# Delta stage of a two-layer block: order of the last output-gate projections and of the work beside them

## The reference, cut to what matters

```
qkv = silu(short_conv([q, k, v]))            # 8 heads, 128 wide each
o   = chunk_gated_delta(q, k, v, g, beta)    # forwards, and backwards
o   = rmsnorm(o_fwd + o_bwd, norm_w)
y_a = o * silu(z)                            # z: the output gate of the head
merged = sigmoid(gate_a) * (y_a @ w_pa) + sigmoid(gate_b) * (y_b @ w_pb)
```

## Time and profile before

| | us |
|---|---|
| runs: median of 3 (lowest to highest) | 3124.99 (3123.63 to 3127.92) |
| the profiled execution, its own time | 3120.17 |
| its span in the trace | 3118.3 |
| TensorE busy / VectorE / ScalarE / GpSimd in the span | 2972.4 / 1687.0 / 1468.2 / 423.7 |
| mean granted TensorE clock | 0.982 of full speed |

### The profile page before, as it was taken

How to read it: one execution, slowest core, us unless ns; L and a number is a source line. 1 busy time by engine, 2 the same in 40 slices (tenths; PEclk the granted TensorE clock), 3 DMA queues, 4 the chain that set the end, 5 groups by cost and what they waited for, 6 DMA issues and landing times. The chain is left out here.

```text
span 3118.3 us, 51224 instructions
## 1 busy us (share of the span) xinstructions
PE 2972.4 (95%) x20348; PEld 2380.8 (76%) x20348; DVE 1687.0 (54%) x2566; ACT 1468.2 (47%) x2859; POOL 423.7 (14%) x276
## 2 busy tenths in 40 slices
PE   7999989999999999899999989989999899899998
PEld 5788777777777788687777867777888777678887
DVE  6767743677447777625766445544344445444343
ACT  4555542656334555425665345644333356543332
POOL 1544510000014545300000000010000100010000
PEclk9999999999999999999999999989999999999999
DMA  3221112212222211122222222113222222122222
GB/s 133 76 74 67 47 62 96 73 59 71 84 88 78 83 62 64 41 94 74 71 71 78 95 65 98 48 55 106 97 94 94 81 72 75 36 93 94 94 95 80
DMA packets 41244, 243.12 MB, mean 78 GB/s; under 512 B 6672, under 2 KB 7632, under 8 KB 15440
## 3 DMA queue, kind: packets, MB, share of 16 engines
q1 hardware_dynamic: 41040, 240.30, 22.3%
HBM read 233.36 MB, written 2.20 MB: 76 GB/s over the span
## 5 line engine op out<-in xcount | busy, mean ns | idle before, releaser
L317 PE MATMUL bank<-hT,ws 128*128 128x512 f32 x2112 | 875.1, 414 | 38.1 <-DVE hT L508 26.0
L321 PE MATMUL bank<-hT,ws 128*128 128x512 f32 x2112 | 830.0, 393 | 0.0
L320 PE MATMUL bank<-hT,ws 128*128 128x512 f32 x2112 | 828.4, 392 | 0.0
L317 PEld LDWEIGHTS bank<-hT,ws 128*128 128x128 f32 x2112 | 400.4, 190 | 126.4 <-issue 48.0
L274 DVE TENSOR_TENSOR ws<-raw,ws 128x2048 fp32r<-128x2048 f32 x160 | 368.5, 2303 | 211.2 <-ACT ws L268 208.2
L268 ACT ACTIVATE ws<-raw 128x2048 fp32r<-128x2048 f32 x172 | 328.9, 1912 | 302.9 <-PE bank L317 181.7
L321 PEld LDWEIGHTS bank<-hT,ws 128*128 128x128 f32 x2112 | 399.0, 189 | 87.6
L320 PEld LDWEIGHTS bank<-hT,ws 128*128 128x128 f32 x2112 | 401.0, 190 | 69.1 <-issue 1.4
L946 PE MATMUL bank<-uS,ws 128*128 128x512 f32 x512 | 199.2, 389 | 0.0
L949 PE MATMUL bank<-uS,ws 128*128 128x512 f32 x512 | 199.2, 389 | 0.0
L950 PE MATMUL bank<-uS,ws 128*128 128x512 f32 x512 | 199.2, 389 | 0.0
(11 more groups left out here) (368 smaller groups left out, 4856.0 us busy)
## 6 DMA issues: line engine op xcount, KB each, us to landing
raw<-in_w_ff SPq DMA_DIRECT2D x64, 1024.0 KB, 4.7
raw<-in_w_delta SPq DMA_DIRECT2D x32, 1024.0 KB, 4.8
raw<-in_w_diff SPq DMA_DIRECT2D x32, 1024.0 KB, 4.8
raw<-in_w_att SPq DMA_DIRECT2D x20, 1024.0 KB, 4.8
raw<-in_w_merge_a SPq DMA_DIRECT2D x16, 1024.0 KB, 4.8
raw<-in_w_merge_b SPq DMA_DIRECT2D x16, 1024.0 KB, 4.8
raw<-in_w_out SPq DMA_DIRECT2D x16, 1024.0 KB, 5.0
rows<-sum_rows SPq DMA_DIRECT2D x16, 512.0 KB, 5.7
```

What stands on the lines that cost most here:

```text
L317: first = pe.matmul(out, hi, x[:, 0, k], start=(begin and k == steps[0]), stop=False)
L320: pe.matmul(out, hi, x[:, 1, k], start=False, stop=False)
L321: last = pe.matmul(out, lo, x[:, 0, k], start=False, stop=(end and k == steps[-1]))
```

## The change

It orders the 32 tiles of a layer anew: z of head 6 and z of head 7 become the last two, so that position 27 is q of head 7, 28 its k, 29 its v, 30 is z of head 6 and 31 z of head 7. The chunks of weights are packed on the host in this order, and waits and banks go by position (`DELTA_AT`). `ahead` is now 3 in cores 0 to 4, 2 in core 5, 1 in core 6, 0 in core 7. The fill of core 5 becomes 24 steps (v of head 6, q and k of head 7), that of core 6 stays at 16 (v of head 7, z of head 6), and that of core 7 begins with 8 steps of z of head 7. The first gate's steps then come in calls 9 to 16, calls 17 to 25 are empty, and the second gate has 26 to 33.

ScalarE applies Silu to z of head 6 in core 6 and not in core 5, and to z of head 7 in core 7, after level 3, between two loads of a table. The splits of the merge stage's first chunks move from level 0 to 2 on ScalarE and from level 1 to 3 on VectorE, in cores 6 and 7; in core 6 two steps of the convolution take the place at level 1.

```diff
+def delta_tiles():
+    tiles = [(h, j) for h in range(HEADS) for j in range(4)]
+    late = [(HEADS - 2, 3), (HEADS - 1, 3)]
+    return [x for x in tiles if x not in late] + late
+DELTA_TILES = delta_tiles()
+DELTA_AT = {hj: n for n, hj in enumerate(DELTA_TILES)}
...
+GATES_PAUSE = 8
...
-                core(i, i % 2, first=(i == 0), ahead=min(2, HEADS - 1 - i))
+                core(i, i % 2, first=(i == 0), ahead=min(3, HEADS - 1 - i))
...
                 def stream(i, ahead):
-                    if ahead:
+                    if ahead > 2:
                         yield from gemm(i + 1, (2, 3))
-                    if ahead > 1:
                         yield from gemm(i + 2, (0, 1))
-                    if not ahead:
+                    elif ahead > 1:
+                        yield from gemm(i + 1, (2, 3))
+                        yield from gemm(i + 2, (0,))
+                    elif ahead:
+                        yield from gemm(i + 1, (1, 2))
+                    else:
+                        yield from gemm(i, (3,))
                         yield from gates_ahead()
...
                         if x == KT - 1:
-                            for _ in range(2 * KT - 1):
+                            for _ in range(GATES_PAUSE):
                                 yield
...
-                        if a == 0:
-                            if ahead > 1:
-                                st.high(act, i + 2, 0)
-                            elif ahead:
-                                following.first_high(act, st)
-                            else:
-                                following.second_high(act)
+                        if a == 0 and ahead > 1:
+                            st.high(act, i + 2, 0)
+                        elif a == 2 and ahead == 1:
+                            following.first_high(act, st)
+                        elif a == 2 and not ahead:
+                            following.second_high(act)
...
                         if a == 3 and ahead:
                             decay_exp(i + 1)
                             act.preload_act_table_set(SILU)
+                        elif a == 3:
+                            act.preload_act_table_set(SILU)
+                            silu_z(i, p)
+                            act.preload_act_table_set(LN_EXP)
                     if ahead:
-                        silu_z(i + 1, 1 - p)
+                        if ahead > 2:
+                            silu_z(i + 1, 1 - p)
+                        elif ahead == 1:
+                            silu_z(i, p)
                         silu(i + 1, 1 - p, 0)
...
                             elif ahead:
-                                following.first_low(dve, st)
-                            else:
-                                following.second_low(dve)
+                                some(fill, 2)
...
-                            some(fill, 2)
+                            if ahead == 1:
+                                following.first_low(dve, st)
+                            elif not ahead:
+                                following.second_low(dve)
+                            else:
+                                some(fill, 2)
```

More of the change, by code:

```diff
@@ L380, in weight_chunks @@
             at = i * P
-            d.append(tile_pair(column_tile(w, (COL_QA + at, P)), column_tile(w, (COL_KA + at, P))))
-            d.append(tile_pair(column_tile(w, (COL_VA + at, P)), column_tile(w, (COL_ZA + at, P))))
             f.append(tile_pair(column_tile(w, (COL_QB + at, P)), column_tile(w, (COL_KB + at, P))))
@@ L386, in weight_chunks @@
             mb.append(tile_pair(column_tile(w, (COL_GB + at, P)), column_tile(pb, (at, P))))
+        tiles = [column_tile(w, ((COL_QA, COL_KA, COL_VA, COL_ZA)[j] + h * P, P)) for h, j in DELTA_TILES]
+        d += [tile_pair(tiles[n], tiles[n + 1]) for n in range(0, len(tiles), 2)]
         for n in range(0, KT, 2):
@@ L1440, in _, with gemm @@
                 st.credit(pe)
-                def gemm(h, js):
+                def gemm(g, js):
                     for j in js:
                         if j % 2 == 0:
-                            st.ready(pe, h, j // 2)
-                        if h > 0 or j >= 2:
-                            pe.wait_ge(taken, h * 4 + j - 1)
+                            st.ready(pe, g, j // 2)
+                        if g > 0 or j >= 2:
+                            pe.wait_ge(taken, g * 4 + j - 1)
                         for last in st.product(pe, B[j % 2][:, :], j // 2, j % 2, k.hT):
@@ L1665, in pad_copy @@
                 def pad_copy(h, j):
-                    act.wait_ge(tile, h * 4 + j + 1)
+                    n = DELTA_AT[h, j]
+                    act.wait_ge(tile, n + 1)
                     if h > 0:
                         act.wait_ge(conv_ready, (h - 1) * 3 + j + 1)
-                    act.activation(pad[:, j, 2:2 + SEQ], B[j % 2][:, :], ACT.Copy).then_inc(taken, 1)
+                    act.activation(pad[:, j, 2:2 + SEQ], B[n % 2][:, :], ACT.Copy).then_inc(taken, 1)
                 def silu(h, p, j):
@@ L1677, in silu_z @@
                 def silu_z(h, p):
-                    act.wait_ge(tile, h * 4 + 4)
-                    act.activation(zs[:, p], B[1][:, :], ACT.Silu).then_inc(taken, 1)
+                    n = DELTA_AT[h, 3]
+                    act.wait_ge(tile, n + 1)
+                    act.activation(zs[:, p], B[n % 2][:, :], ACT.Silu).then_inc(taken, 1)
                 def token_squares(h, p, j, core):
@@ L1840, in conv @@
                     for j in range(3):
-                        dve.wait_ge(taken, h * 4 + j + 1)
+                        dve.wait_ge(taken, DELTA_AT[h, j] + 1)
                         chain(dve.tensor_scalar(cv[:, j], pad[:, j, 0:SEQ], cw[:, j, 0:1], None, ALU.mult))
@@ L1872, in gate_out @@
                     dve.wait_ge(x_ready, scratch_use(use, core) + 1)
-                    dve.wait_ge(taken, h * 4 + 4)
+                    dve.wait_ge(taken, DELTA_AT[h, 3] + 1)
                     dve.scalar_tensor_tensor(yt, B[XB][:, :], pA[:, PA_GNW:PA_GNW + 1], zs[:, p], ALU.mult, ALU.mult).then_inc(x_taken, 1)
```

## The result

The median went from 3124.79 us (15 runs) to **3130.63 us** (15 runs, 3126.24 to 3138.06): a ratio of 1.0021, with a 95% interval of 1.0015 to 1.0028. The forecast was 3130.5 us. The change made the kernel slower: by 5.8 us or 0.19% between the medians, just inside the 0.2% that the prediction called no change.

A forecast was written before the change was run, and what follows sets the result against it. TensorE bounds cores 1 to 5, latency between VectorE, ScalarE and TensorE the thin stretches of cores 6 and 7. Per layer -1.5 + 0 + 4.2 = +2.7 us, +5.5 for two, gives 3130.5 us; range 3121 to 3138.

The forecast's parts named there:

- Core 5: Core 5 loses eight product steps and becomes 1.5 us shorter per layer, between 0 and 2.4.
- The wait on GpSimd: Core 5's tail: N waits behind GpSimd's low part and L1364, with 0.4 us in hand, so it costs nothing.
- Core 6: Core 6 keeps 16 steps; the moved split stays covered by product steps: 0, with 0.3 us either way.
- Core 7: Core 7 per layer: beginning 2.5 us longer, `widen` of level 4 1.95 later, L1601 of s = 1 0.25 sooner: 4.2 longer.
- The fourth merge step after the transposes: End of core 7: one merge step more follows the last transposes; adds 0, at most 0.4 us.
- the 0.25: Core 7: call 25 becomes empty, so L1601 of s = 1 goes when r is ready, 0.25 us sooner.
- The clock: TensorE's half-clock falls in thin stretches: filled levels 1 to 3 against thinner level 4 and core 5 tail cancel, 4 us either way.
- The slow rival: Core 7's level 4 stall loses the clock in both layers, plus a fall in core 5's tail: 3136.3 us; chance 0.30.
- The fall that it gave to core 5's tail: Part of the slower rival: a clock fall of 1.3 us in core 5's thin tail.
- The sign of being wrong: Half-clock stretches outweigh the terms of the sum; one of three signs named, no size given.
- The drain: Rival: each table switch in core 7 costs a 1.38 us drain beside its load, 5.6 us in all: 3136.1 us; chance 0.03.
- the fast rival: Filled levels keep the clock up in core 7 of both layers, 9.0 us back: about 3119.7 us; chance 0.12.

The follow-up runs named there:

- the idle products in the stall: The changed kernel with six 128x512 matmuls whose result nobody reads in the level 4 stall of core 7: 3126.8 us, 1.0008 of the kernel before.
- the row with four loads: The changed kernel with two more table loads behind the two at level 3 of core 7: 3138.7 us, 1.0041 of the kernel before.
- the loads moved: The changed kernel with Silu of z of head 7 and its two table loads moved to s = 2 of core 7: 3123.3 us, 0.9998.
- core 6 with 24 steps: The new tile order with core 5's eight steps moved to core 6, core 7 that of the kernel before: 3120.5 us, 0.9989.
- core 7 with thin levels: The kernel before, but core 7 has one product step before and one after `widen`, second gate straight after the first: 3118.8 us, 0.9974.

## Why the prediction was right

The forecast of 3130.5 us and the median of 3130.63 agree to 0.1 us, and that closeness is luck. The mechanism was right, but the terms of the sum were 1.1 us per layer too low together, and no run shows what made up for it.

**Core 5: -1.5 us forecast, -1.6 measured.** The bound from core 6's tail and the two ScalarE operations that core 6 lacks were the right ingredients. The wait on GpSimd was closer than the 0.4 us given. One of VectorE's small operations took 1.91 us and ended as GpSimd's low part did; N was ready 0.16 us ahead of its transposes (355.18 and 0.69, against 356.03). VectorE, layer 0, then TensorE:

```profile
350.71 1.91 DVE L1883 TENSOR_SCALAR odd<-odd 128x4 f32<-128x4 f32 x1
...
355.18 0.69 DVE L1936 TENSOR_TENSOR Nn<-Nn,cc 128x512 f32<-128x512 f32 x1
...
356.03 0.60 PE L1567 MATMUL bank<-cc,Nn 128*128 128x128 f32 x4
```

**Core 6: 0 forecast, +0.8 measured.** This is the term that was mis-sized, outside its 0.3. I weighed TensorE's cover for the moved split and not what GpSimd reads beside it.

**Core 7: 2.5 + 1.95 - 0.25 = 4.2 forecast, +4.6 at full clock** (48.96 with the idle products in the stall, against 44.33). The beginning is 19.50 us for 19.48, `widen` comes 3.81 us after its level for 3.8. Of the missing 0.4, some 0.26 lie at the end: from the start of VectorE's last low part to the merge stage it takes 1.80 us in the run with idle products for 1.54 (443.69 to 445.23). The fourth merge step after the transposes was given as 0 to 0.4 and taken as 0. The rest is the 0.25: L1601 of s = 1 did come that much sooner, but only 0.10 of it was left at the last transposes.

**The clock: taken as cancelling within 4 us.** This held, and not for want of falls. By the first three terms the change costs 2 x (-1.6 + 0.8 + 4.6) = 7.6 us; 5.8 were measured. The interval of 4.7 to 8.7 us holds both, and where the 1.8 between them lie stays open. The slow rival's mechanism was real: level 4's stall goes with a fall in both layers, 3.5 and 2.0 us, and in all 6 profiled windows that have it; idle products in it give 3.8 us back. What the rival left out is that the kernel before loses some 4.3 us in the same core. The fall that it gave to core 5's tail came in 1 of 16 windows with 24 steps there. The sign of being wrong, half-clock stretches that outweigh the terms, didn't come: in core 7 they cost 5.5 us in the changed kernel's profiled execution and 4.5 in the one before, and the difference is far below 7.6. I had seen one such fall in one execution and could not tell how often it comes.

**The rivals.** The drain is refuted by the row with four loads. That the filled levels keep the clock (the fast rival) was right for levels 1 to 3 and useless, for the fall comes behind level 4; with the loads moved it came true, and the kernel drew level with the one before. Added up, the bounds that the prediction quotes for its forecast give 3124.7 to 3137.5 us and not 3124 to 3135; nothing else in it hangs on that.

## What to carry to other kernels

Moving cover from one latency-bound stretch to another pays by the gap that each step hides, so price both ends from rows: here eight steps of 6.2 us gave back 1.6 us where they left, cost 1.5 in level 4, the last block and s = 0 of core 6, and 2.5 in levels 1 to 3 of core 7. A wait that holds TensorE in a thin stretch is to be priced twice, once for itself and once for the clock behind it, and an activation that needs another table belongs where its engine waits anyway. Put the steps first where a gap is about as long as a step: eight of them cost 1.0 us in the levels and the last block of core 7, and 2.5 in its recurrence, whose gaps are 0.2 to 0.55 us.

## What the runs showed of the hardware

TensorE's clock fell to half of full speed (1.2 of 2.4 GHz) without any wait of TensorE longer than about 1 us before it: in core 6 with waits of 0.74 and 0.97 us, in core 7 of the kernel before in 4 of 6 windows. The two cores whose levels and last block have a product step in nearly every gap never lost it in the profiled executions, though their recurrences hold no step (core 6 with 24 steps, core 7 with thin levels: 8 of 8 windows at 1.00). The Trainium skill (TensorE: Matmul & The Clock Gate, "A second HAM failure mode") tells of short idle times between groups of matmuls that make the clock swing; the traces agree.

GpSimd and VectorE slowed each other when both read two tiles from SBUF: 2.96 us for 1.42, 1.64 for 0.69, and three convolution steps 3.64 for 2.33. The Trainium skill (GPSIMD Engine Reference, "1. Specifications") says that GpSimd shares its SBUF interfaces with VectorE and contends with instructions that have two SBUF inputs; the traces agree, and in the one run that shifted GpSimd's operations the collision only moved.
